# Down projection of the prompt's rows as seven products of halves in two passes, its weight sums shared by GpSimd and VectorE

## The reference, cut to what matters

```python
    h = rmsnorm(x, norm_ffn_g)
    gt, ffn_buf_new = causal_dwconv(h @ w_gate, ffn_buf, ffn_conv_w)
    x = x + (jax.nn.silu(gt) * (h @ w_up)) @ w_down      # w_down: 2816 x 1024
```

## Time and profile before

| | us |
|---|---|
| median of 3 runs | 945.5 |
| lowest and highest | 945.16, 945.92 |
| span of the profiled execution | 943.7 |
| TensorE busy in it | 931.8 (99%) |
| VectorE, ScalarE, GpSimd busy | 648.3, 452.1, 170.0 |

### The profile page before, as it was taken

The page is one execution under the profiler, slowest core; times in us unless marked ns, Lnnn a source line. Parts: engine busy times, 40 slices in busy tenths (PEclk is TensorE's granted clock), DMA queues, the critical chain, the costliest instruction groups (busy, mean ns, idle before and its releaser), DMA issues.

```text
span 943.7 us, 16891 instructions
## 1 busy us (share of the span) xinstructions
PE 931.8 (99%) x6919; PEld 841.9 (89%) x6919; DVE 648.3 (69%) x1083; ACT 452.1 (48%) x836; POOL 170.0 (18%) x198
## 2 busy tenths in 40 slices
PE   9999999999999999999999999999999999999998
PEld 7899888998889877799888999999999999888886
DVE  7627888777775565552666999999999999435321
ACT  6634454648566454554654445444444445333310
POOL 0071101103664331000002032222222220000000
PEclk9999999999999999999999999999999999999999
DMA  8624142121104084244904322222222224412221
GB/s 303 225 88 145 54 168 93 47 94 49 45 5 135 2 290 154 82 142 157 317 18 138 113 87 90 90 90 90 88 73 74 79 89 152 147 64 93 78 89 56
DMA packets 73820, 103.70 MB, mean 110 GB/s; under 512 B 2576, under 2 KB 53904, under 8 KB 73360
## 3 DMA queue, kind: packets, MB, share of 16 engines
q1 hardware_dynamic: 73744, 102.63, 32.6%
HBM read 92.27 MB, written 10.35 MB: 109 GB/s over the span
## 4 chain that ended last, share of the span: by engine, by line
PE 51%; DVE 3%; ACT 2%; POOL 1%; issue 1%; ACTq 0%; POOLq 0%; DVEq 0%
PE bank L1222 8%; PE bank L1220 8%; PE bank L1221 8%; PE bank L538 5%; PE bank L537 5%; PE bank L536 5%; PE bank L484 2%; PE bank L486 1%; PE bank L485 1%; PE bank L466 1%; PE bank L562 1%; PE bank L1034 1%; PE bank L564 1%; PE bank L563 1%; PE bank L1036 1%
## 5 line engine op out<-in xcount | busy, mean ns | idle before, releaser
L2168 DVE TENSOR_TENSOR wlo<-wraw,whi 128x2048 fp32r<-128x2048 f32 (+1 forms) x56 | 126.2, 2253 | 102.2 <-ACT whi L1617 93.0
L1617 ACT ACTIVATE whi<-wraw 128x2048 fp32r<-128x2048 f32 (+1 forms) x58 | 109.3, 1885 | 101.9 <-PE bank L538 72.8
L498 PE MATMUL bank<-hhi,whi 128*128 128x320 f32 x352 | 116.4, 331 | 0.6 <-issue 0.6
L500 PE MATMUL bank<-hhi,wlo 128*128 128x320 f32 x352 | 108.7, 309 | 0.0
L499 PE MATMUL bank<-hlo,whi 128*128 128x320 f32 x352 | 108.7, 309 | 0.0
L498 PEld LDWEIGHTS bank<-hhi,whi 128*128 128x128 f32 x352 | 66.2, 188 | 5.0 <-issue 3.6
L499 PEld LDWEIGHTS bank<-hlo,whi 128*128 128x128 f32 x352 | 66.2, 188 | 3.0 <-issue 2.4
L500 PEld LDWEIGHTS bank<-hhi,wlo 128*128 128x128 f32 x352 | 66.1, 188 | 0.0
L536 PE MATMUL bank<-whi,hhi 128*128 128x512 f32 x150 | 58.4, 389 | 0.0
L537 PE MATMUL bank<-wlo,hhi 128*128 128x512 f32 x150 | 58.4, 389 | 0.0
L538 PE MATMUL bank<-whi,hlo 128*128 128x512 f32 x150 | 58.3, 389 | 0.0
(11 more groups left out here) (491 smaller groups left out, 2690.4 us busy)
## 6 DMA issues: line engine op xcount, KB each, us to landing
wraw<-in_w_in SPq DMA_DIRECT2D x13, 1024.0 KB, 5.5
wraw<-in_w_gate SPq DMA_DIRECT2D x11, 1024.0 KB, 5.2
wraw<-in_w_up SPq DMA_DIRECT2D x11, 1024.0 KB, 5.1
wraw<-in_w_down SPq DMA_DIRECT2D x10, 1024.0 KB, 5.1
kTs<-in_cache_sb_k SPq DMA_DIRECT2D x8, 512.0 KB, 4.4
vraw<-in_cache_sb_v SPq DMA_DIRECT2D x8, 512.0 KB, 4.9
wraw<-in_w_mix_out SPq DMA_DIRECT2D x4, 1024.0 KB, 6.3
kmT<-in_cache_mem_k SPq DMA_DIRECT2D x8, 512.0 KB, 6.2
```

The lines of the kernel that those rows point to most:

```text
L498: T.matmul(o, wh[:, k, cs], hhi[:, k, hs], start=(k == 0), stop=False)
L500: ins = T.matmul(o, wl[:, k, cs], hhi[:, k, hs], start=False, stop=(k == KD - 1))
L1617: V(wv(whi, i), wv(wraw, i), ACT.Copy).then_inc(s["w_hi_ready"], 1)
L2168: V.tensor_tensor(wv(wlo, i), wv(wraw, i), wv(whi, i).bitcast(F32), ALU.subtract)\
```

## The change

The 512 prompt rows times the 2816 x 1024 weights are done as one step of a fast multiplication with seven products of halves instead of eight. The halves are: prompt rows 0 to 255 and 256 to 511; features 0 to 10 and 11 to 21 (HF = 11 pieces each); output columns 0 to 511 and 512 to 1023. The sample's 128 rows are multiplied in the plain way ("cs"). The work goes in two passes over the 11 pairs of feature pieces (i, HF + i), and w_down is read from HBM twice, in 22 blocks of 1 MB; block d holds pieces i and HF + i with all 1024 columns.

- **First pass**, i = 0 to 10: products p1, p3 and p5 for two row tiles each, and the sample's rows in two banks: 6 + 12 + 6 + 6 = 30 matmuls a step. All eight banks are held until the end of the pass. GpSimd makes the sums of `act` for the pair (`first_sums`, four operations of 256 columns) and one weight sum (`t1_sum`, 512 columns); VectorE makes one more sum of `act` inside `parts_lo`; ScalarE and VectorE split parts, weights and t1.
- **Second pass**: products p6, p7, p4 and p2 for two row tiles each, 24 matmuls a step. Three weight sums are made in place in the loaded block: two by GpSimd (`block_sums`), the third by VectorE (`fourth_sum`), after which ScalarE cuts. The last two pairs are done product by product.
- **Between them** ScalarE copies the banks of p1 to SBUF and VectorE's `first_rows` empties the other six, both at d == HF + 2 in their order; `more_rows` adds the p1 and p1+p5 sums to xres in d = 14 to 17; `last_rows` adds the four last products.
- Four buffers `dn_raw0` to `dn_raw3` take the blocks (`dn_lo` lies on top of `dn_raw`); block d is loaded when PE has passed block d-4. `part_hi`/`part_lo` have six slots, `t1` three.

```diff
-            down("dn", 0, B_DN[0], left_a, NT, ready_a)
-            down("dn", 1, B_DN[1], left_a, NT, ready_a)
+            for i in range(HF):
+                pe.wait_ge(s["parts_lo"], i + 1)
+                lo_cut(pe, B_DN[i])
+                product("p1", i, dn_parts(i, 0), dn_weights(i, 0, 0))
+                samples(i)
+                product("p3", i, dn_parts(i, 512), dn_weights(i, 1, 1))
+                pe.wait_ge(s["t1_lo"], i + 1)
+                ins = product("p5", i, dn_parts(i, 256), (t1_hi[t1_slot(i)][:, :], t1_lo[t1_slot(i)][:, :]))
...
+            SECOND = (("p6", 0, 0, 0), ("p7", 256, 0, 1), ("p4", 768, 1, 1), ("p2", 512, 1, 0))
...
+            for i in range(HF - 2):
+                d = HF + i
+                pe.wait_ge(s["parts_lo"], d + 1)
+                lo_cut(pe, B_DN[d])
+                for name, p0, a, c in SECOND:
+                    ins = product(name, i, dn_parts(d, p0), dn_weights(d, a, c))
+                step(ins, B_DN[d])
...
+            def load_w(i):    # on SP; d = i - B_DN[0]
...
+                    if d == 3:
+                        filled(sp, (("up", FT // 2 - 1), "p5"))
+                    else:
+                        passed(sp, i - 3 if d < 3 else i - 4)
...
+            def first_sums(i):    # on GpSimd
+                raw, left, right = part_raw[part_slot(i)], act[:, i, 0:512], act[:, HF + i, 0:512]
+                part_free(pool, i)
+                act_made(pool, i)
+                G.tensor_tensor(raw[:, 256:512], left[:, 256:512], right[:, 256:512], ALU.add)
+                link(G.tensor_tensor(raw[:, 512:768], left[:, 0:256], right[:, 0:256], ALU.add))
+                G.tensor_tensor(left[:, 256:512], left[:, 0:256], left[:, 256:512], ALU.subtract)
+                G.tensor_tensor(raw[:, 512:768], raw[:, 512:768], raw[:, 256:512], ALU.subtract).then_inc(s["part_sums"], 1)
...
+            def block_sums(d):
...
+                dn_ready(pool, d)
+                link(G.tensor_tensor(b12, b22, b12, ALU.subtract))
+                G.tensor_tensor(b11, b12, b11, ALU.add).then_inc(s["block_sums"], 1)
...
+            for i in range(HF):
+                first_sums(i)
+                t1_sum(i)
+            for d in range(HF, 2 * HF):
+                block_sums(d)
...
+            def fourth_sum(d):    # on VectorE
...
+                dve.wait_ge(s["block_sums"], d - HF + 1)
+                V.tensor_tensor(w[:, 1, 512:D_MODEL], w[:, 0, 0:512], w[:, 1, 0:512], ALU.subtract)\
+                    .then_inc(s["fourth_sums"], 1)
...
+            for d in range(1, 2 * HF):
+                if d == HF:
+                    fourth_sum(d)
+                if HF <= d < 2 * HF - 1:
+                    fourth_sum(d + 1)
+                cut_lo(B_DN[d])
+                parts_lo(d)
+                if d < HF:
+                    t1_low(d)
+                if d == HF + 2:
+                    first_rows()
...
+                if HF + 3 <= d < HF + 7:
+                    more_rows(d - HF - 3)
+            last_rows()
```

More of the change, by code:

```diff
@@ L59 @@
 DEEP = 4
-FIRST = 3
 WARM = 18
-LEAD = 2
 SEVEN = {"gate": range(2, 11), "up": range(1, 11)}
@@ new lines, in dn_parts, with dn_weights, samples @@
+            def dn_parts(m, c):
+                hi, lo = part_hi[part_slot(m)], part_lo[part_slot(m)]
+                return hi, lo, c
+            def dn_weights(d, a, c):
+                cs = slice(512 * c, 512 * c + 512)
+                return wv(whi, B_DN[d])[:, a, cs], wv(wlo, B_DN[d])[:, a, cs]
+            def samples(i):
+                hi, lo = part_hi[part_slot(i)], part_lo[part_slot(i)]
+                for c in range(2):
+                    if i == 0:
+                        take(("cs", c))
+                    o = bank[use["cs", c][0]][:, :]
+                    for a in range(2):
+                        ss = slice(768 + a * P, 768 + a * P + P)
+                        wh, wl = dn_weights(i, a, c)
+                        T.matmul(o, hi[:, ss], wh, start=(i == 0 and a == 0), stop=False)
+                        T.matmul(o, hi[:, ss], wl, start=False, stop=False)
+                        ins = T.matmul(o, lo[:, ss], wh, start=False, stop=(i == HF - 1 and a == 1))
+                    if i == HF - 1:
+                        done(ins, ("cs", c))
@@ L2125, in _ @@
                     first_copy("up", j, u1)
+                cut_hi(28 + 2 * j)
                 if j == FT // 2 - 1:
-                    for n in range(LEAD):
-                        act_hi(n)
-                cut_hi(28 + 2 * j)
+                    cut_parts(0)
+                    cut_t1(0)
                 for c in range(2):
@@ L2811, in _ @@
                 if j == FT // 2 - 1:
-                    for n in range(LEAD):
-                        act_lo(n)
+                    parts_lo(0)
+                    t1_low(0)
                 if j in SEVEN["up"]:
@@ new lines, in free, with first_rows @@
+            def free(ins, name, t):
+                ins.then_inc(bank_free[use[name, t][0]], 1)
+            def first_rows():
+                dve.wait_ge(s["rows_back"], 16)
+                for c in range(2):
+                    free(to_rows("cs", c, PT, c), "cs", c)
+                for t in range(2):
+                    free(to_rows("p3", t, t, 1), "p3", t)
+                for t in range(2):
+                    evacuated(dve, ("p1", t))
+                    b = filled(dve, ("p5", t))
+                    V.tensor_tensor(sum_p15[:, t, :], sum_p1[:, t, :], bank[b][:, :], ALU.add).then_inc(bank_free[b], 1)
```

258 lines of the change are left out of this document (191 added, 67 removed).

## The result

The changed kernel takes **978.44 us** (median of 4 runs, 975.92 to 979.25); the kernel before, on the same chip, 945.33 (944.80 to 945.92). The ratio is 1.0345, with a 95% interval of 1.0331 to 1.0360: slower by 33 us. The profiled execution has a span of 977.5 us, for 943.7 before.

The account below looks back on a forecast made before the run. The prediction took TensorE's issue rate to bound the kernel. Its terms, -15.0 + 16 + 11.3 + 13 = +25.3 us on 945.5, gave 970.8 us, own range 964 to 977, 8-in-10 range 946 to 979.

Parts of the forecast that it names:

- The matmuls removed: Down projection: 594 matmuls stand for 660, each issued every 0.2267 us; -15.0 us.
- Part 2, the first pass: First pass: VectorE and GpSimd take turns on SBUF inputs, a step needing 8.1 us for TensorE's 6.80; +16 us.
- The entry: Start of the first pass: GpSimd's sums for pair 2 delay `cut_lo(1)` and `parts_lo(1)` by 3 to 5 us; 4 us.
- the steps: First pass: 10 steps, each 1.2 us longer because VectorE and GpSimd take turns; 12 us.
- Part 3, the queue: Between the passes: bank 3 waits behind `fourth_sum(14)`, which waits for GpSimd's sums and block 14's load; +11.3 us.
- Part 4, the second pass: Second pass: blocks have a short lead, VectorE and GpSimd take turns, and the end adds 2.7; +13 us.
- the turns: Second pass: VectorE and GpSimd alternating make a block 6.7 us on the mean, 8 x 1.3 = 10 us.
- The clock: Rival: TensorE's clock halves after the long middle wait, slowing 18 to 40 matmuls; +5, 975.8 us, chance 0.15.
- What costs nothing: ScalarE's early cuts, reading xres back and the second pass's loads are hidden, and the tail stays, +-0.5 us.
- the signs named: Right: TensorE waits in both passes, about 11 us before bank 3, slow GpSimd operations. Wrong: clock below full, among others.
- The rival "no hindrance": VectorE and GpSimd do not hinder each other in this stage; -15.0 + 0 + 11.3 + 6 = +2.3, 947.8 us, chance 0.17.

Follow-up runs that it names:

- e2: Changed kernel with GpSimd's sums cut to 8 columns and left out of the result, instructions, waits and order kept; 944.58 us.
- e5: Changed kernel with the first pass's GpSimd sums moved to VectorE from the third pair on; 968.47 us.
- e6: Changed kernel with all the stage's GpSimd sums except pair 1's on VectorE, and `first_rows` ahead of `fourth_sum(14)`; 947.71 us.
- e1: Changed kernel with `first_rows` ahead of `fourth_sum(14)` on VectorE and ScalarE's copies of p1 one block earlier; 969.24 us.
- e4: Changed kernel with 24 further matmuls on TensorE ahead of p7 in block 11, filling the wait for the bank; 976.64 us.
- e8: e6 with the split of the second pass's three weight sums put back, two on GpSimd and one on VectorE; 954.85 us.
- e10: e6 with block 11's sums ahead of `t1_low(10)` and `first_rows` at d == HF + 1, all weight sums on VectorE; 945.23 us.

## Why the prediction was right, and where not

- **The matmuls removed** (-15.0): 594 matmuls at 0.2267 us. Right; in e2, e5 and e6 the steps without a wait are 6.80 and 5.44 us, within 0.03.
- **Part 2, the first pass** (+16 predicted): 14.6 us, of which 2.4 late start, 3.8 wait in front of block 1, 5.5 in seven steps, 2.9 in front of block 10. The mechanism is right: steps of 7.68 us for the 8.1 worked out, set by VectorE's stretched list, and e5 takes it away. One thing was not seen. GpSimd's sums for pair 0 already meet VectorE in up block 10, whose convolutions read two SBUF operands (0.83 to 1.78 us for 0.75), and `parts_lo(0)` is hindered too: hence the late start, and a wait of 3.65 us at 803.74. The entry was put too low (4 for 6.2) and the steps too high (12 for 8.4), so that the sum came near is luck in part.
- **Part 3, the queue** (+11.3): 10.3 us in two waits, 3.8 for the copies of p1 by ScalarE and 6.5 for bank 3. The chain was the one predicted, link by link; e1 undid it. The prediction had ScalarE's lateness inside the one wait, and so it was in sum.
- **Part 4, the second pass** (+13): 9.8 us of waits, 2.3 of them the last block's. Mis-sized: the turns were laid over all eight steps, but in those of blocks 12, 18 and 19 (5.44 to 5.57 us) they cost TensorE nothing, and the mean of the others did not make up for it.
- **The clock**, at nothing in the sum, is the step that failed: 11.7 us, the largest error. The rival had the mechanism, and its 975.8 is the nearest of all the numbers named, but it tied the fall to the one long wait of the middle and priced it at 5, for 18 to 40 matmuls, a count that no run shows (5 to 13 behind each wait here, 56 in all). The clock fell behind seven waits, most of them of the kind that the prediction itself had forecast in parts 2 and 4. Once waits of 2.5 to 4 us stand in a sum, their clock belongs in the sum. The Trainium skill, "TensorE: Matmul & The Clock Gate", section "Why this matters for your kernels", advises against idle gaps of TensorE between bursts of matmuls. The trace agrees in kind (0.50 behind the wait at 803.74), but the length of a wait alone does not tell: 2.37 us in e5 was followed by half the clock, 3.25 us in e4 and 3.08 in e8 were not.
- **What costs nothing**: the tail is 3.6 us as before. The reload of xres shows in no wait.
- **The sum**: -15.0 + 14.6 + 10.3 + 9.8 + 11.7 + 2.5 (lateness behind waits, and spread) = 33.9 us, for 25.3 predicted. The three waits were together 5.6 too high, the clock and its like 14.2 too low. The forecast's range (964 to 977) ends 1.4 us below the 978.44, which lies just inside the top of the wide one (946 to 979). Of the signs named, the waits at each step of the first pass (0.9 to 1.2 us from start to start), GpSimd's 2.79 us and the second pass's waits came as said; in the middle two waits came for one of 11 us; and the granted clock below full, named as a sign of being wrong, came too.
- **The rival "no hindrance"** (947.8): e2 made its world, and took GpSimd's own time out of the chains besides, and gave 944.58. GpSimd's sums are thus the whole loss. That it is by hindering VectorE is shown by VectorE's durations, by the first pass of e5 and by e8; how much of the rest is GpSimd's own time in the chain to `fourth_sum` was not told apart. How much of the loss is left if VectorE makes all the sums but those of pair 1 is e6: 947.7.

What stays open: how the 2.0 us wait in front of block 1 of e5 to e10 could go, and whether `more_rows`, which costs VectorE 4 x 1.2 us while it is the bound, can be hidden. Neither was tried. Open too is what decides whether the clock falls behind a wait of 2.4 to 3.3 us.

## What to carry to other kernels

Two engines that hinder each other, as VectorE and GpSimd do here with SBUF inputs, count as one engine: add their work before laying it against the step, and give the second engine only what fits beside the first one's PSUM work or its idle time. An operand sum that VectorE does in 0.7 us is not relieved by a GpSimd that needs 1.3 us of the same turns. Banks that the next phase needs are emptied ahead of any work that waits for a load; and a forecast wait of TensorE of a few us may need a second term, for the matmuls at half the clock behind it.
